# Expert jobs of 64 rows or fewer: the low parts of the activations beside the high parts

## The chip, the cores and the metric

One core of a Trainium2 chip runs the whole program. The metric is device time of one execution in microseconds, the median over runs. The matrix engine is TensorE (PE), the vector engine VectorE (DVE), the activation engine ScalarE (ACT), GpSimd is POOL, and SyncE (SP) issues the weight DMAs. Each engine has a sequencer that takes waits, branches and register loads and hands the rest to the engine's queue; the trace marks the sequencer's own instructions with a q (PEldq, DVEq).

## The reference

One decoder layer on x of 1 x 1024 x 1024 in float32: a combined projection, latent attention and differential attention, gates, an output projection, then a routed expert layer and a final norm. The change touches only the expert layer:

```
logits = t @ w_router + b_router;  top 4 of 32 experts for each of 1024 tokens
hcat = x_rows @ w1[e] + b1[e]                      # 1024 -> 2048
act  = min(glu, 7) * sigmoid(1.702 * glu) * (clip(lin) + 1)
y    = (act @ w2[e] + b2[e]) * weight of the row   # 1024 -> 1024
out[token] += y
```

Each expert has 4 MB in each half of w1 and 4 MB in w2, all in float32. For the reference's own inputs the router gives the 32 experts these numbers of rows, in order of size: 358, 240, 239, 227, 213, 196, 189, 183, 174, 170, 156, 136, 126, 124, 110, 110, 105, 100, 96, 92, 92, 91, 91, 81, 72, 68, 66, 56, 39, 35, 31, 30.

## The kernel before

`stage_experts` runs last. Its work is cut into jobs of one expert and up to 256 rows (JOB); the expert with 358 rows makes a second job of 102, so there are 33. The router's stage sorts them by rows, largest first, and writes tables that the engines read in their loops (`job_expert`, `job_count`, `job_place`). A job of more than 128 rows (P) is wide, the others are narrow: 12 wide jobs run first, then 21 narrow ones. Each engine loops over the jobs on its own, reads the counts into registers (`value_load`), and branches into a wide or a narrow body.

Weights. SP fills six slots of 2 MB for the next job (`load_weights`, lines 1817 to 1829). Slots 0 to 3 hold w1: slot c has 256 columns of the glu half and 256 of the linear half (s = 0 and 1), in two DMAs of 1 MB with rows of 1 KB. Slots 4 and 5 hold the halves of w2's columns, in one DMA of 2 MB each with rows of 2 KB. Each slot has one buffer: SP waits for the current job to be done with it (line 1915 for w1, by PE's count `made`, which rises eight times a job; line 1917 for w2, by `w_lo_ready`, which rises when DVE has split one of eight pieces of w2).

A narrow job on PE (`job`, line 2012). First projection, `first_narrow`: for c of 0 to 3 and s of 0 and 1, 16 plain float32 products with 128 columns, which the trace shows as 32 matmuls each, 256 in all. Its results go to the banks 2*(c%2)+s. Then eight transposes of the next job's rows (`turn_x`). Then the second projection with each operand split into a high and a low part (type fp32r): act_hi x w_hi, act_lo x w_hi and act_hi x w_lo, each of 16 matmuls 128x512, 48 in all, in eight pieces q of six (q 0 to 3 to bank 0, q 4 to 7 to bank 2). All matmuls take 128 stationary columns, however many rows the job has. A wide job does the same in 384 matmuls of 256 columns for the first projection and 96 or, at 192 rows (MID) or fewer, 80 for the second; those of 192 or fewer skip with a branch at each q (line 2054).

The pieces of w2. For each q ACT writes the high part (`high`, line 2119) and DVE the low part (`low`, line 2232). In a narrow job they go to six places (`narrow_slots[q % 6]`), so q 6 and 7 need the places of q 0 and 1: ACT waits on `piece_used`, which PE raises by one when it is through with q 0 and by one when through with q 1 (line 2062). PE waits before each q for `w_lo_ready` (line 2039), and at q 3 for the fourth `act_lo_ready`, which DVE gives when the low part of the last quarter of the activations is there (line 2271).

The end of a narrow job (`whole`): DVE scales bank 0 into yg, ACT scales bank 2, POOL scatters yg to the accumulated rows. PE's next job waits for `yg_dve` and `yg_act` before it writes the banks again (line 2022). After the last job, rows are read back, normed and stored.

Of the kernel before, what the change touches and what calls it, by code (L numbers as in the profile page):

```python
# [25 lines left out]
ALU = mybir.AluOpType  # L26
# [3 lines left out]
P = 128  # L30
# [1779 lines left out]

def weight_slots(g):

    return ([at(g, R + c * RING_SLOT, RING_SLOT).rearrange("p (s k n) -> p s k n", s=2, k=KT) for c in range(4)],
            [tiled(g, R + (4 + c) * RING_SLOT, FT, HALF) for c in range(2)])


def load_weights(g, io, eng, expert, slot):

    w1, w2 = weight_slots(g)
    if slot < 4:  # L1820
        src = io.w1.rearrange("e (k p) n -> p e k n", p=P)
        for s in range(2):
            col = s * D_EXP + slot * 2 * P
            eng.dma_start(w1[slot][:, s].unsqueeze(1), src[:, bass.ds(expert, 1), :, col:col + 2 * P]).then_inc(g.w_in[slot], 16)
    else:
        src = io.w2.rearrange("e (k p) n -> p e k n", p=P)
        col = (slot - 4) * HALF
        eng.dma_start(w2[slot - 4].unsqueeze(1), src[:, bass.ds(expert, 1), :, col:col + HALF]).then_inc(g.w_in[slot], 16)
# [28 lines left out]
def stage_experts(g, io):  # L1857
# [24 lines left out]
    first_of = lambda p: w1[p // 4][:, p // 2 % 2, :, p % 2 * P:(p % 2 + 1) * P]  # L1882
# [12 lines left out]
    with nc.Block() as block:  # L1895

        @block.sync
        def _(sp):
            sp.wait_ge(gathered, 32)
            for slot in (2, 3):  # L1900
                load_weights(g, io, sp, 0, slot)
            sp.wait_ge(scattered, 16 * TT)
            for slot in (4, 5):
                load_weights(g, io, sp, 0, slot)
            total = sp.value_load(g.total[0:1, 0:1], min_val=EXPERTS, max_val=JOBS)
            with sp.Fori(1, JOBS) as n:
                with sp.If(total > n):
                    expert = sp.value_load(g.job_expert[0:1, bass.ds(n, 1)], min_val=0, max_val=EXPERTS - 1)
                    for c in range(6):

                        if c < 4:
                            sp.wait_ge(made, 8 * n + (2 * c - 6))
                        else:
                            sp.wait_ge(w_lo_ready, 8 * n + (4 * c - 20))
                        load_weights(g, io, sp, expert, c)
                with sp.Else():
                    sp.nop()

# [65 lines left out]
        def _(pe):  # L1984
# [8 lines left out]
            def first_narrow(n, c, s):  # L1993
                for a in range(2):
                    for k in range(KT):
                        last = nc.tensor.matmul(bank(g, 2 * (c % 2) + s)[:, a * JOB:a * JOB + P], w1[c][:, s, k, a * P:(a + 1) * P],  # L1996
                                                xt[:, k, 0:P], start=(k == 0), stop=(k == KT - 1))
                last.then_inc(made, 1)

# [9 lines left out]
                        last.then_inc(slot_used.sem, 1)  # L2009
                last.then_inc(made, 1)  # L2010

            def job(n, wide, count, next_count):
                pe.wait_ge(xt_dve, 2 * n + 2)
                pe.wait_ge(xt_act, 4 * n + 4)
                for c in range(4):
                    pe.wait_ge(g.w_in[c], 32 * n + 32)
                    if c >= 2:
                        pe.wait_ge(act_ready, 4 * n + (c - 1))
                    for s in range(2):

                        if c < 2:
                            pe.wait_ge((yg_dve, yg_act)[c], 2 * n + (s + 1))
                        (first_wide if wide else first_narrow)(n, c, s)

                pe.wait_ge(gathered, 32 * n + 64)
                with pe.If(next_count > P):
                    turn_x(2)
                with pe.Else():
                    turn_x(1)


                halves = 2 if wide else 1

                if wide:
                    pe.sem_inc(piece_used, 2)
                pe.wait_ge(act_lo_ready, 4 * n + 3)
                for c in range(2):
                    for q in range(4 * c, 4 * c + 4):
                        pe.wait_ge(w_lo_ready, 8 * n + (q + 1))
                        if q == 3:  # L2040
                            pe.wait_ge(act_lo_ready, 4 * n + 4)
                        def second(h, x, y):
                            for a in range(2):
                                f = 2 * (q % 4) + a
                                last = nc.tensor.matmul(bank(g, 2 * c + h), x[:, f, h * P:(h + 1) * P], second_part(q, wide)[:, y, a, :],  # L2045
                                                        start=(f == 0 and x is act_hi and y == 0), stop=(f == FT - 1 and x is act_hi and y == 1))
                            return last

                        for h in range(halves):
                            second(h, act_hi, 0)  # L2050
                            if h == 0:
                                second(h, act_lo, 0)
                            else:
                                with pe.If(count > MID):
                                    second(h, act_lo, 0)
                            last = second(h, act_hi, 1)
                            if q % 4 == 3:
                                last.then_inc(y_made, 3 - halves)
                            elif wide and h == 1:
                                last.then_inc(slot_used.sem, 1)  # L2060
                            elif not wide and q < 2:
                                last.then_inc(piece_used, 1)

            pe.wait_ge(gathered, 32)
            turn_x(2)
# [1 line left out]
            with nc.Fori(0, JOBS, engines=[mybir.EngineType.PE], hint_back_edge=True) as n:  # L2067
                with pe.If(total > n):
                    count = pe.value_load(g.job_count[0:1, bass.ds(n, 1)], min_val=0, max_val=SEQ)
                    next_count = pe.value_load(g.job_count[0:1, bass.ds(n + 1, 1)], min_val=0, max_val=SEQ)  # L2070
                    with pe.If(count > P):
                        job(n, True, count, next_count)
                    with pe.Else():
                        job(n, False, count, next_count)
                with pe.Else():
                    pe.nop()

# [15 lines left out]
        def _(act):  # L2093
# [25 lines left out]
                nc.scalar.activation(second_part(q, wide)[:, 0], piece_of(q), ACT.Copy).then_inc(w_hi_ready, 1)  # L2119

            def first_high(n, p):
                if p % 4 == 0:
                    act.wait_ge(g.w_in[p // 4], 32 * n + 32)
                if p >= 4:
                    first_free(act, n, p - 4)
                nc.scalar.activation(first_part[p][:, 0], first_of(p), ACT.Copy).then_inc(v_hi_ready.sem, 1)  # L2126

            def job(n, wide, count, next_count):
# [43 lines left out]
                        nc.scalar.activation(yg[:, h, HALF:], bank(g, 2 + h), ACT.Copy, scale=weight(n, h)).then_inc(yg_act, 1 if wide else 2)  # L2172

                if not wide:
                    whole(1)
                    return
                with act.If(count > MID):
                    next_high()
# [34 lines left out]
        def _(dve):  # L2213
# [24 lines left out]
            def job(n, wide, count, next_count, expert):  # L2238
# [9 lines left out]
                for c in range(4):  # L2248
# [24 lines left out]
                    if wide:  # L2273
                        with dve.If(count > MID):
                            low_act(act_lo[:, fs, 0:JOB], slice(0, JOB)).then_inc(act_lo_ready, 1)
                        with dve.Else():
                            low_act(act_lo[:, fs, 0:P], slice(0, P))
                            low_act(act_hi[:, fs, MID:JOB], slice(P, MID)).then_inc(act_lo_ready, 1)
                    else:
                        low_act(act_lo[:, fs, 0:P], slice(0, P)).then_inc(act_lo_ready, 1)  # L2280
                    if not wide and c < 3:
                        low(n, 2 * c, False)
                        low(n, 2 * c + 1, False)
# [38 lines left out]
                        dve.wait_ge(yg_dve, 2 * n + 4)  # L2322
                        dve.sem_inc(low_added.sem, 1)
                else:
                    whole(1)
                    dve.sem_inc(low_added.sem, 2)

            dve.sem_inc(yg_dve, 2)
            first_low(0, 0)
# [81 lines left out]
```

## Time and profile before

| | |
|---|---|
| three runs | 2834.12, 2828.44, 2836.38 us; median 2834.12 us |
| the profiled execution | 2832.55 us, of which the span of the trace is 2830.9 us |
| PE busy | 2680.1 us, 95% of the span |
| DVE, ACT, POOL busy | 53%, 38%, 11% |
| granted clock of PE, mean | 0.975 of full |
| DMA | 527.28 MB, mean 186 GB/s |
| expert layer | from about 1121 us to about 2805 us; wide jobs to 1949 us, narrow jobs to 2797 us |

A matmul's duration in the trace holds its way through the array; the next one starts before it ends. What one costs in a stream is the distance between starts: the length of a piece of the chain of waits divided by its count. Every time is in us from the start of the span. In the timeline, "x48" merges 48 instructions, and the brackets at a row's end give the engine's idle time before it and what ended it.

### The profile page before, as it was taken

The page shows a single profiled execution, that of the slowest core. Times are in us where ns is not written, and L with a number is a line of the kernel's source. Part 1 is how long each engine was busy: PE and PEld are TensorE (multiplying, and loading weights), DVE is VectorE, ACT ScalarE, POOL GpSimd, SP SyncE. Part 2 cuts the span into 40 slices and gives each one's busy share as a digit, 9 for nine tenths or more (in the row PEclk, how much of TensorE's full clock was granted, in tenths as well). Part 3 has the DMA queues.
Part 4 walks back from the last instruction along what each step waited for, and adds up shares of the span by engine and source line. Part 5 has one row for each costly group of instructions (what it writes and reads, how often), then busy time and mean ns, then how long its engine had stood idle before and what let it go on. Part 6 is the DMA issues. An engine that isn't in the chain of part 4 may idle for free.

```text
span 2830.9 us, 46350 instructions
## 1 busy us (share of the span) xinstructions
PE 2680.1 (95%) x16420; PEld 2218.6 (78%) x16421; DVE 1503.9 (53%) x2641; ACT 1068.2 (38%) x1684; POOL 309.1 (11%) x327
## 2 busy tenths in 40 slices
PE   7899989979999997999999999999999999999995
PEld 3356655556666555899999999999999999999994
DVE  5545436764111246666666777775445544454444
ACT  2144324443110123545555555554333333333333
POOL 1000000000000124101111111110111211112111
PEclk9999989999999997999999999999999999999997
DMA  4000010002111552966666677767999999999995
GB/s 141 0 10 5 16 31 16 1 1 67 45 44 44 194 100 78 322 216 208 207 207 207 209 220 228 231 213 246 349 348 344 337 342 344 342 336 342 344 343 169
DMA packets 424683, 527.28 MB, mean 186 GB/s; under 512 B 27844, under 2 KB 334536, under 8 KB 424584
## 3 DMA queue, kind: packets, MB, share of 16 engines
q1 hardware_dynamic: 403544, 464.31, 50.6%
q0 software_dynamic: 20032, 62.11, 9.3%
q8 instruction: 37, 0.61, 0.1%
q14 instruction: 30, 0.25, 0.0%
q10 hardware_dynamic: 1040, 0.00, 0.0%
HBM read 482.23 MB, written 44.14 MB: 186 GB/s over the span
## 4 chain that ended last, share of the span: by engine, by line
PE 59%; DMA 1%; issue 0%; ACT 0%; SPq 0%; DVE 0%; POOLq 0%; POOL 0%; ACTq 0%
PE banks L1996 21%; PE banks L2006 20%; PE banks L2045 17%; PE banks L1988 1%; DMA arena<-acc_rows 0%; DMA acc_rows<-arena,rows 0%; ACT parts L2099 0%; SPq L1923 0%; DVE arena L2351 0%; ACT arena L2208 0%; ACT parts L2126 0%; ACT arena L2172 0%; POOLq L1949 0%; POOL acc_rows L1943 0%; ACT stat L2210 0%
## 5 line engine op out<-in xcount | busy, mean ns | idle before, releaser
L1996 PEld LDWEIGHTS banks<-arena 128*128 128x128 f32 x5376 | 603.5, 192 | 1.7
L1996 PE MATMUL banks<-arena 128*128 128x128 f32 x5376 | 603.7, 275 | 0.0
L2006 PE MATMUL banks<-parts 128*128 128x256 f32 x4608 | 558.6, 284 | 7.2 <-issue 7.2
L2006 PEld LDWEIGHTS banks<-parts 128*128 128x128 f32 x4608 | 557.9, 193 | 8.8 <-issue 8.0
L2045 PE MATMUL banks<-parts 128*128 128x512 f32 x2064 | 476.8, 391 | 0.0
L2045 PEld LDWEIGHTS banks<-parts 128*128 128x128 f32 x2064 | 385.1, 188 | 78.5
L2232 DVE TENSOR_TENSOR parts<-arena,parts 128x1024 fp32r<-128x1024 f32 x264 | 315.2, 1222 | 118.2 <-ACT parts L2119 118.0
L2255 DVE TENSOR_SCALAR arena<-banks,arena 128x128 f32<-128x128 f32 (+1 forms) x528 | 181.3, 392 | 317.6 <-PE banks L1996 314.0
L2236 DVE TENSOR_TENSOR parts<-arena,parts 128x1024 fp32r<-128x1024 f32 x192 | 233.6, 1224 | 183.9 <-ACT parts L2126 183.4
L2119 ACT ACTIVATE parts<-arena 128x1024 fp32r<-128x1024 f32 x264 | 269.2, 1055 | 77.4 <-PE banks L2006 43.4
L2126 ACT ACTIVATE parts<-arena 128x1024 fp32r<-128x1024 f32 x192 | 201.8, 1057 | 173.2 <-PE banks L2006 117.1
L1329 PE MATMUL banks<-parts 128*128 128x512 f32 x768 | 178.8, 393 | 0.0
L1329 PEld LDWEIGHTS banks<-parts 128*128 128x128 f32 x768 | 144.2, 188 | 33.3 <-issue 3.8
L2147 ACT ACTIVATE parts<-arena 128x256 fp32r<-128x256 f32 (+1 forms) x132 | 65.6, 497 | 257.5 <-DVE arena L2263 252.7
L2143 ACT ACTIVATE arena<-arena 128x256 f32<-128x256 f32 (+1 forms) x132 | 65.3, 495 | 229.9 <-DVE arena L2255 229.9
L1973 POOL COPY rows<-entries 128x2 int32 x33 | 6.0, 182 | 1092.3 <-ACT arena L2172 799.4
L1562 PE MATMUL banks<-arena 128*128 128x512 f32 x256 | 115.2, 609 | 6.0 <-PEq L1280 3.2
L1404 DVE TENSOR_TENSOR arena<-banks,arena 128x512 f32<-128x512 f32 x32 | 20.6, 686 | 184.1 <-ACT arena L1360 184.1
L1943 POOL DMA_INDIRECT acc_rows<-arena,rows x66 | 108.4, 1642 | 66.2 <-issue 66.2
L1321 PE MATMUL banks<-arena 128*128 128x512 f32 x256 | 111.3, 592 | 1.5 <-DVE arena L1384 1.5
L1562 PEld LDWEIGHTS banks<-arena 128*128 128x128 f32 x256 | 49.2, 195 | 66.9 <-issue 63.2
L1321 PEld LDWEIGHTS banks<-arena 128*128 128x128 f32 x256 | 48.5, 190 | 59.7 <-issue 59.2
(313 smaller groups left out, 2724.8 us busy)
## 6 DMA issues: line engine op xcount, KB each, us to landing
arena<-in_w SPq DMA_DIRECT2D x264, 1024.0 KB, 7.7
arena<-in_w SPq DMA_DIRECT2D x66, 2048.0 KB
arena<-in_w_in SPq DMA_DIRECT2D x27, 512.0 KB, 5.4
arena<-in_x SPq DMA_DIRECT2D x16, 512.0 KB, 7.0
h_rows<-arena POOLq DMA_DIRECT2D x10, 512.0 KB, 8.5
acc_rows<-arena SPq DMA_DIRECT2D x8, 512.0 KB, 5.3
arena<-acc_rows SPq DMA_DIRECT2D x8, 512.0 KB, 6.7
out<-arena SPq DMA_DIRECT2D x8, 512.0 KB, 6.8
```

Source lines behind the costliest of these rows:

```text
L1321: nc.tensor.matmul(bank(g, 4 * h + b), w[s][b][:, k, :], yt[:, k0 + k, cols], start=(k == 0), stop=(k == 3))
L1329: last = nc.tensor.matmul(bank(g, 4 * h + b), w_parts[:, s, c, b, k, :], part[:, k, cols], start=(k == 0 and c == 0 and part is h_hi), sto ...
L1562: last = nc.tensor.matmul(bank(g, 2 * (t % 2) + h), merged[:, k, t * P:(t + 1) * P], w_out[:, k, h * HALF:(h + 1) * HALF], start=(k == 0), ...
L1943: pool.indirect_dma_start(out=io.acc, out_offset=bass.IndirectOffsetOnAxis(ap=rows_out[0:rows, h:h + 1], axis=0), in_=yg[0:rows, h, :], in ...
L1996: last = nc.tensor.matmul(bank(g, 2 * (c % 2) + s)[:, a * JOB:a * JOB + P], w1[c][:, s, k, a * P:(a + 1) * P], xt[:, k, 0:P], start=(k == ...
L2006: last = nc.tensor.matmul(bank(g, 2 * (c % 2) + s)[:, a * JOB:(a + 1) * JOB], first_part[p][:, y, k, :], x[:, k, :], start=(k == 0 and y = ...
L2045: last = nc.tensor.matmul(bank(g, 2 * c + h), x[:, f, h * P:(h + 1) * P], second_part(q, wide)[:, y, a, :], start=(f == 0 and x is act_hi ...
L2119: nc.scalar.activation(second_part(q, wide)[:, 0], piece_of(q), ACT.Copy).then_inc(w_hi_ready, 1)
L2126: nc.scalar.activation(first_part[p][:, 0], first_of(p), ACT.Copy).then_inc(v_hi_ready.sem, 1)
L2232: nc.vector.tensor_tensor(part[:, 1], piece_of(q), part[:, 0], ALU.subtract).then_inc(w_lo_ready, 1)
L2236: nc.vector.tensor_tensor(first_part[p][:, 1], first_of(p), first_part[p][:, 0], ALU.subtract).then_inc(v_lo_ready.sem, 1)
L2255: nc.vector.tensor_scalar(dst[:, a, 0:w], bank(g, 2 * (c % 2) + s)[:, a * JOB:a * JOB + w], b1_t[:, bass.ds(expert, 1), s * FT + 2 * c + a ...
```

## The change

For narrow jobs of 64 rows or fewer, DVE writes the low parts of the activations into columns 64 to 127 of act_hi, which no row of the job uses. One pass act_hi x w_hi then gives hi x w_hi in the upper 64 output rows and lo x w_hi in the lower 64, act_hi x w_lo likewise, and ACT and DVE add the two halves at the end. The 16 matmuls act_lo x w_hi are skipped by a branch on the count, once for each half of the columns (at q 3 and q 7); for narrow jobs of 65 to 128 rows they run there, all eight of a half together. `piece_used` now rises by two, at q 3. The narrow body of PE no longer reads or tests the next job's count. w1's slots now hold 512 columns of one half of w1 each, with rows of 2 KB, and the waits on the slots follow.

```diff
-            col = s * D_EXP + slot * 2 * P
-            eng.dma_start(w1[slot][:, s].unsqueeze(1), src[:, bass.ds(expert, 1), :, col:col + 2 * P]).then_inc(g.w_in[slot], 16)
+        col = slot % 2 * D_EXP + slot // 2 * HALF
+        for ks in (slice(0, KT // 2), slice(KT // 2, KT)):
+            eng.dma_start(w1[slot][:, ks].unsqueeze(1), src[:, bass.ds(expert, 1), ks, col:col + HALF]).then_inc(g.w_in[slot], 16)
...
-                            sp.wait_ge(made, 8 * n + (2 * c - 6))
+                            sp.wait_ge(made, 8 * n + (4 * (c // 2) + c % 2 - 5))
...
-                    pe.wait_ge(g.w_in[c], 32 * n + 32)
                     for s in range(2):
+                        if c % 2 == 0:
+                            pe.wait_ge(g.w_in[c + s], 32 * n + 32)
...
-                with pe.If(next_count > P):
-                    turn_x(2)
-                with pe.Else():
+                if wide:
+                    next_count = pe.value_load(g.job_count[0:1, bass.ds(n + 1, 1)], min_val=0, max_val=SEQ)
+                    with pe.If(next_count > P):
+                        turn_x(2)
+                    with pe.Else():
+                        turn_x(1)
+                else:
                     turn_x(1)
...
+                        if not wide:
+                            if q % 4 == 3:
+                                with pe.If(count > P // 2):
+                                    for r in range(4 * c, 4 * c + 4):
+                                        second(c, 0, r, act_lo, 0)
+                            last = second(c, 0, q, act_hi, 0)
+                            if q == 3:
+                                last.then_inc(piece_used, 2)
+                            last = second(c, 0, q, act_hi, 1)
+                            if q % 4 == 3:
+                                last.then_inc(y_made, 2)
+                            continue
...
-                            elif not wide and q < 2:
-                                last.then_inc(piece_used, 1)
...   ACT, end of a narrow job
-                    whole(1)
+                    with act.If(count > P // 2):
+                        whole(1)
+                    with act.Else():
+                        for c in range(2):
+                            act.wait_ge(y_made, 4 * n + (2 * c + 2))
+                            nc.scalar.activation(low_sums[:, c * HALF:(c + 1) * HALF], bank(g, 2 * c)[P // 2:P], ACT.Copy).then_inc(yg_act, 1)
...   DVE, low parts of the activations
+                        with dve.If(count > P // 2):
+                            low_act(act_lo[:, fs, 0:P], slice(0, P)).then_inc(act_lo_ready, 1)
+                        with dve.Else():
+                            low_act(act_hi[:, fs, P // 2:P], slice(0, P // 2)).then_inc(act_lo_ready, 1)
...   DVE, end of a narrow job of 64 rows or fewer
+                        dve.wait_ge(yg_act, 2 * n + 3)
+                        nc.vector.tensor_tensor(low_sums[:, 0:HALF], low_sums[:, 0:HALF], bank(g, 0)[rows], ALU.add).then_inc(yg_dve, 1)
+                        dve.wait_ge(yg_act, 2 * n + 4)
+                        nc.vector.tensor_tensor(low_sums[:, HALF:], low_sums[:, HALF:], bank(g, 2)[rows], ALU.add).then_inc(low_added.sem, 1)
...
+                        nc.vector.tensor_scalar(yg[rows, 0, :], low_sums, weight(n, 0)[rows], None, ALU.mult).then_inc(yg_dve, 1)
```

## Rows read from the trace of the kernel before

**Rows 1.** The page: the whole span, and its costliest groups on PE.
```profile
span 2830.9 us, 46350 instructions
L1996 PE MATMUL banks<-arena 128*128 128x128 f32 x5376 | 603.7, 275 | 0.0
...
L2045 PE MATMUL banks<-parts 128*128 128x512 f32 x2064 | 476.8, 391 | 0.0
```

**Rows 2.** The chain that ended last, in order: start us, us, what.
```profile
1883.89 46.07 PE banks L2006 x384
1930.84 18.17 PE banks L2045 x80
...
2272.18 28.58 PE banks L1996 x256
2301.64 10.90 PE banks L2045 x48
2312.54 28.58 PE banks L1996 x256
```

**Rows 3.** Timeline of PE from 2300: start us, us, line, count.
```profile
2300.60 1.04 PE L1988 MATMUL banks<-ident,arena 128*128 128x128 f32 x8
2301.39 11.15 PE L2045 MATMUL banks<-parts 128*128 128x512 f32 x48
2312.38 28.75 PE L1996 MATMUL banks<-arena 128*128 128x128 f32 x256
```

**Rows 4.** Timelines of ACT and of DVE in the same job.
```profile
2303.68 2.02 ACT L2119 ACTIVATE parts<-arena 128x1024 fp32r<-128x1024 f32 x2
2312.73 0.69 ACT L2172 ACTIVATE arena<-banks,entries 128x512 f32<-128x512 f32 x1 [7.03 <-PE banks L2045]
...
2304.78 2.36 DVE L2232 TENSOR_TENSOR parts<-arena,parts 128x1024 fp32r<-128x1024 f32 x2 [0.89 <-ACT parts L2119]
2307.31 0.75 DVE L2304 TENSOR_SCALAR arena<-banks,entries 128x512 f32<-128x512 f32 x1 [0.17 <-PE banks L2045]
```

**Rows 5.** PE's sequencer, lines 2067 to 2071, 2022, 2041: ns min/median/max, first to last start.
```profile
L2067 PEldq ALU_OP  x1: 32/32/32, 2308.6 to 2308.6; - x1
L2070 PEldq FUSED_REGOPS  x2: 51/104/156, 2310.1 to 2310.6; - x2
L2071 PEldq COMPARE_BRANCH  x1: 216/216/216, 2310.9 to 2310.9; - x1
L2022 PEldq ALU_OP  x1: 32/32/32, 2311.5 to 2311.5; - x1
L2041 PEldq EVENT_SEMAPHORE  x2: 51/51/51, 2303.3 to 2343.6; - x2
```

**Rows 6.** PE at the second wide job's start, and its sequencer.
```profile
1203.31 1.14 PEld L2006 LDWEIGHTS banks<-parts 128*128 128x128 f32 x5 [5.37 <-issue]
L2003 PEldq FUSED_REGOPS  x1: 37/37/37, 1203.2 to 1203.2; - x1
L2003 PEldq ALU_OP  x4: 32/32/32, 1204.8 to 1215.2; - x4
```

**Rows 7.** Branches of PE's sequencer over the whole span.
```profile
L2054 PEldq COMPARE_BRANCH  x96: 71/148/218, 1175.3 to 1944.3; - x96
L2071 PEldq COMPARE_BRANCH  x45: 75/189/6157, 1124.0 to 2754.8; - x45
```

**Rows 8.** DMA from 2304 to 2308, from 2352 to 2356, and from 2300 to 2360.
```profile
DMA packets 1415, 1.43 MB, mean 358 GB/s; under 512 B 16, under 2 KB 1415, under 8 KB 1415
...
DMA packets 770, 1.54 MB, mean 386 GB/s; under 512 B 16, under 2 KB 16, under 8 KB 770
q0 software_dynamic: 395, 1.23, 8.0%
```

**Rows 9.** Timeline of SP from 2300: the weight DMAs.
```profile
2302.11 5.56 SPq L1828 DMA_DIRECT2D arena<-in_w  x2
2319.86 22.43 SPq L1824 DMA_DIRECT2D arena<-in_w  x8
```

**Rows 10.** End of a wide job of 192 rows or fewer, and POOL after a narrow job.
```profile
1883.93 0.59 ACT L2186 ACTIVATE arena<-banks 64x512 f32<-64x512 f32 x1
1884.56 1.28 DVE L2317 TENSOR_TENSOR arena<-arena,banks 64x512 f32<-64x512 f32 x2 [0.57 <-ACT arena L2186]
1885.97 0.74 DVE L2321 TENSOR_SCALAR arena<-arena,entries 64x1024 f32<-64x1024 f32 x1
1886.88 0.19 POOL L1973 COPY rows<-entries 128x2 int32 x1 [49.06 <-DVE arena L2321]
...
2313.64 0.18 POOL L1973 COPY rows<-entries 128x2 int32 x1 [24.00 <-ACT arena L2172]
```

**Rows 11.** The first job: DMA from 1131 to 1136, and ACT's wait for slot 3.
```profile
q0 software_dynamic: 244, 0.87, 87.0%
q1 hardware_dynamic: 245, 0.25, 17.8%
...
1156.92 2.01 ACT L2126 ACTIVATE parts<-arena 128x1024 fp32r<-128x1024 f32 x2 [2.09 <-DMA arena<-in_w]
```

More of the change, by code:

```diff
@@ L1811, in weight_slots @@
 def weight_slots(g):
-    return ([at(g, R + c * RING_SLOT, RING_SLOT).rearrange("p (s k n) -> p s k n", s=2, k=KT) for c in range(4)],
+    return ([tiled(g, R + c * RING_SLOT, KT, HALF) for c in range(4)],
             [tiled(g, R + (4 + c) * RING_SLOT, FT, HALF) for c in range(2)])
@@ L1821, in load_weights @@
         src = io.w1.rearrange("e (k p) n -> p e k n", p=P)
-        for s in range(2):
-            col = s * D_EXP + slot * 2 * P
-            eng.dma_start(w1[slot][:, s].unsqueeze(1), src[:, bass.ds(expert, 1), :, col:col + 2 * P]).then_inc(g.w_in[slot], 16)
+        col = slot % 2 * D_EXP + slot // 2 * HALF
+        for ks in (slice(0, KT // 2), slice(KT // 2, KT)):
+            eng.dma_start(w1[slot][:, ks].unsqueeze(1), src[:, bass.ds(expert, 1), ks, col:col + HALF]).then_inc(g.w_in[slot], 16)
     else:
@@ L1881, in stage_experts @@
     first_part = [slots[p % 4].rearrange("p (s k n) -> p s k n", s=2, k=KT) for p in range(W1_PIECES)]
-    first_of = lambda p: w1[p // 4][:, p // 2 % 2, :, p % 2 * P:(p % 2 + 1) * P]
+    w1_cols = lambda c, s, a: w1[2 * (c // 2) + s][:, :, (c % 2 * 2 + a) * P:(c % 2 * 2 + a + 1) * P]
+    first_of = lambda p: w1_cols(p // 4, p // 2 % 2, p % 2)
     second_part = lambda q, wide: (slots[q % 4] if wide else narrow_slots[q % 6]).rearrange("p (s f n) -> p s f n", s=2, f=2)
@@ L1995, in first_narrow @@
                     for k in range(KT):
-                        last = nc.tensor.matmul(bank(g, 2 * (c % 2) + s)[:, a * JOB:a * JOB + P], w1[c][:, s, k, a * P:(a + 1) * P],
+                        last = nc.tensor.matmul(bank(g, 2 * (c % 2) + s)[:, a * JOB:a * JOB + P], w1_cols(c, s, a)[:, k, :],
                                                 xt[:, k, 0:P], start=(k == 0), stop=(k == KT - 1))
@@ L2010, in first_wide, with job @@
                 last.then_inc(made, 1)
-            def job(n, wide, count, next_count):
+            def job(n, wide, count):
                 pe.wait_ge(xt_dve, 2 * n + 2)
@@ L2036, in job, with second @@
                 pe.wait_ge(act_lo_ready, 4 * n + 3)
+                def second(c, h, q, x, y):
+                    for a in range(2):
+                        f = 2 * (q % 4) + a
+                        last = nc.tensor.matmul(bank(g, 2 * c + h), x[:, f, h * P:(h + 1) * P], second_part(q, wide)[:, y, a, :],
+                                                start=(f == 0 and x is act_hi and y == 0), stop=(f == FT - 1 and x is act_hi and y == 1))
+                    return last
                 for c in range(2):
@@ L2041, in job @@
                             pe.wait_ge(act_lo_ready, 4 * n + 4)
[L2042 to L2047, printed above, removed]
+                        if not wide:
[10 more added lines that the diff above has]
+                            continue
                         for h in range(halves):
-                            second(h, act_hi, 0)
+                            second(c, h, q, act_hi, 0)
                             if h == 0:
-                                second(h, act_lo, 0)
+                                second(c, h, q, act_lo, 0)
                             else:
                                 with pe.If(count > MID):
-                                    second(h, act_lo, 0)
-                            last = second(h, act_hi, 1)
+                                    second(c, h, q, act_lo, 0)
+                            last = second(c, h, q, act_hi, 1)
                             if q % 4 == 3:
-                                last.then_inc(y_made, 3 - halves)
-                            elif wide and h == 1:
+                                last.then_inc(y_made, 1)
+                            elif h == 1:
                                 last.then_inc(slot_used.sem, 1)
-                            elif not wide and q < 2:
-                                last.then_inc(piece_used, 1)
             pe.wait_ge(gathered, 32)
@@ L2069, in _ @@
                     count = pe.value_load(g.job_count[0:1, bass.ds(n, 1)], min_val=0, max_val=SEQ)
-                    next_count = pe.value_load(g.job_count[0:1, bass.ds(n + 1, 1)], min_val=0, max_val=SEQ)
                     with pe.If(count > P):
-                        job(n, True, count, next_count)
+                        job(n, True, count)
                     with pe.Else():
-                        job(n, False, count, next_count)
+                        job(n, False, count)
                 with pe.Else():
@@ L2121, in first_high @@
             def first_high(n, p):
-                if p % 4 == 0:
-                    act.wait_ge(g.w_in[p // 4], 32 * n + 32)
+                if p % 8 in (0, 2):
+                    act.wait_ge(g.w_in[p // 8 * 2 + p % 8 // 2], 32 * n + 32)
                 if p >= 4:
@@ L2279, in job @@
                     else:
-                        low_act(act_lo[:, fs, 0:P], slice(0, P)).then_inc(act_lo_ready, 1)
+                        with dve.If(count > P // 2):
+                            low_act(act_lo[:, fs, 0:P], slice(0, P)).then_inc(act_lo_ready, 1)
+                        with dve.Else():
+                            low_act(act_hi[:, fs, P // 2:P], slice(0, P // 2)).then_inc(act_lo_ready, 1)
                     if not wide and c < 3:
@@ L2324, in job @@
                 else:
-                    whole(1)
-                    dve.sem_inc(low_added.sem, 2)
+                    with dve.If(count > P // 2):
+                        whole(1)
+                        dve.sem_inc(low_added.sem, 2)
+                    with dve.Else():
+                        rows = slice(0, P // 2)
+                        dve.wait_ge(yg_act, 2 * n + 3)
+                        nc.vector.tensor_tensor(low_sums[:, 0:HALF], low_sums[:, 0:HALF], bank(g, 0)[rows], ALU.add).then_inc(yg_dve, 1)
+                        dve.wait_ge(yg_act, 2 * n + 4)
+                        nc.vector.tensor_tensor(low_sums[:, HALF:], low_sums[:, HALF:], bank(g, 2)[rows], ALU.add).then_inc(low_added.sem, 1)
+                        dve.wait_ge(yg_free, n + 1)
+                        dve.wait_ge(yg_dve, 2 * n + 3)
+                        dve.wait_ge(low_added.sem, 2 * n + (low_added.count + 1))
+                        nc.vector.tensor_scalar(yg[rows, 0, :], low_sums, weight(n, 0)[rows], None, ALU.mult).then_inc(yg_dve, 1)
+                        dve.wait_ge(yg_dve, 2 * n + 4)
+                        dve.sem_inc(low_added.sem, 1)
             dve.sem_inc(yg_dve, 2)
```

## The prediction

> **What bounds the kernel now.** I read the page first, then the chain of waits, then the timeline of each engine over one narrow job, then the sequencer's own instructions on PE. The page shows PE's two big narrow groups with no idle time before them [rows 1]. The chain of waits is PE from the first job to the last, with no other engine in it: a narrow job is 28.58 us of first projection, 10.90 us of second, and some 0.9 us of transposes, 40.36 us from start to start, and each piece follows the one before without a hole [rows 2]. So only two things count: matmuls that leave PE, and holes that appear in PE. One matmul of the second projection costs 10.90 / 48 = 0.227 us, 18.17 / 80 in a wide job the same [rows 2].
>
> DMA is no bound, though the share reads full. A narrow job loads 12.58 MB: 8.39 MB in 1 KB rows at 358 GB/s and 4.19 MB in 2 KB rows at 386 GB/s, 23.4 + 10.9 = 34.3 us, and the gathers and scatters take 8.0% of the engines, 3.2 us a job [rows 8]: 37.5 of 40.36 us.
>
> **How many jobs.** The reference's router gives five experts 64 rows or fewer (56, 39, 35, 31, 30). Twelve have more than 128, and the second job of the largest is narrow, so 21 jobs are narrow: 16 of 65 to 128 rows and 5 short ones. The 2064 matmuls of line 2045 agree: 21 x 48 + 6 x 96 + 6 x 80 [rows 1].
>
> **Removed.** Sixteen matmuls in 5 jobs: 5 x 16 x 0.227 = 18.2 us less on PE, all on the path.
>
> **The new wait: pieces 6 and 7.** Before, PE gave back the places of pieces 0 and 1 after 6 and 12 matmuls, and DVE had both low parts done at 2304.78 + 2.36 = 2307.14 [rows 4], 5.75 us after PE began the second projection at 2301.39, while PE wants piece 6 only at matmul 36. Now PE gives both back at q 3: after 14 matmuls in a short job, after 22 in the others (12 + 8 low + 2). I count from PE's start, matmul i at 0.09 + 0.227 i (so the 48th is at 10.76, one step before the next job's first at 10.99 [rows 3]). An engine starts 0.6 us after the start of the matmul that frees it: ACT at 11.34 after the 48th, DVE at 5.92 after the 24th [rows 4]. DVE starts 1.10 after ACT and has both pieces 2.36 later [rows 4]. So the second low part is there at
> - short job: matmul 13 at 3.04, ACT 3.64, DVE 4.74, done 7.10. PE would be at piece 7 (after 28 matmuls) at 6.45.
> - other narrow job: matmul 21 at 4.86, ACT 5.46, DVE 6.56, done 8.92. PE would be there (after 36) at 8.26.
>
> PE's own time for piece 6 fits in between, so the second wait ends last. What is queued behind it is piece 7 and the whole next job.
>
> **What the wait uncovers: PE's sequencer.** Today it runs ahead. It reaches the loop's end at 2308.6, when the array has started 31 of 48 matmuls, so 16 pairs of weight load and matmul stand in the queue; from there to its last step before the next job (2311.5, plus some 0.05) it needs 2.95 us, of which the second count load is 0.8 (2310.1 to 2310.9) [rows 5]. The queue covers 3.6 us, so nothing shows. After a wait that has emptied the array, only what the sequencer hands over afterwards covers the loop. Its pace with an empty queue: 24 pairs between 1203.2 and 1204.8, some 0.0625 us a pair [rows 6] (the queue may have filled in that time, so this is an upper bound there; the bound above it that I keep is 0.11, the array's step in the first projection, 28.58 / 256 [rows 2]). With one load less the loop takes 2.15. A wait takes 0.05 [rows 5], a branch 0.07 not taken and 0.22 taken [rows 7], first weights 0.1 [rows 6].
> - short job: 7.10 + 0.05 + 0.22 + 4 x 0.0625 + 2.15 + 0.1 = 9.87 for the next job's first matmul, against 10.99: 1.12 us gained of the 3.63 removed.
> - other narrow job: 8.92 + 0.05 + 0.07 + 12 x 0.0625 + 2.15 + 0.1 = 12.04: 1.05 us lost. Its array is done at 8.92 + 0.22 + 12 x 0.227 = 11.86, so 0.9 of this is the piece and 0.2 the loop.
>
> The branch at q 3 costs nothing: the sequencer is held there for the fourth act_lo_ready until 2303.3, 1.9 in [rows 5], with some 4 of 12 matmuls still queued (0.9 us), and DVE's new branch before it is of the same size as PE's.
>
> **The end of a short job.** ACT copies 64x512 (0.59), DVE adds (half of 1.28) and scales (0.74) [rows 10]. From the last matmul: 0.6 + 0.6 + 0.04 + 0.68 + 0.05 + 0.75 = 2.7 us until yg_dve rises. PE wants it for s = 1 of the next job, 3.6 us after that job's start, so it hides; if DVE were over 2 us later it would cost the difference. Before, POOL started 1.5 us after the last matmul (2313.64 against 2312.15 [rows 4, 10]); now 2.7 + 0.17 = 2.9. This shows once, after job 33: 1.4 us more there. That job's last matmul comes at 8.15 instead of 10.76, so it gives 2.6 - 1.4 = 1.2.
>
> **Moved at no cost.** In wide jobs the next count is read after the first projection: 0.8 us of sequencer time under 16 queued pairs of 46.07 / 384 = 0.12 us [rows 2], 1.9 us; uncovered it would be at most 12 x 0.8 = 10 us. The test before a narrow job's transposes was covered in the same way, so its going gives nothing. Slots 0 and 2 of w1 are free one step of 3.57 us later, and slots 1 and 3 are wanted one step earlier. SP issued slot 0 at 2319.86, 7.5 us into the job [rows 9]; at 11 it still has 29 us until the next one. With 2 KB rows the weights take 12.58 / 386 = 32.6 us, 35.8 with the software queue, in a period of at least 39.2: the wide rows earn nothing now, and cover the shorter period. Slot 5 is issued 1 to 3 us later than before, behind slots 3 and 4 that are still moving. In the first job slots 2 and 3 share the engines with eight scatters, packet by packet (244 against 245 in 5 us [rows 11]). A 2 KB packet gets more of each turn; slot 3 lands by my estimate at 1151 instead of 1156.9, and ACT wants it at 1149 instead of 1155; PE's piece 10 comes at about 1157. No cost; 0 to 3 us if it lands no sooner.
>
> **Sum.** 16 x 1.05 - 4 x 1.12 - 1.2 = 16.8 - 4.5 - 1.2 = +11.1 us. On the profiled execution: 2832.55 + 11.1 = 2843.7. The median lies 1.6 above that execution, within its runs' spread of 8, so I forecast 2845. Its own range, for 0.3 us either way in a narrow job: 2839 to 2851.
>
> **Rivals.**
> - *The sequencer stays covered* (its loop is hidden in another way than by the queue). Then only pieces delay PE: others 8.92 + 0.22 - 8.26 = +0.88, short jobs 7.10 + 0.37 + 0.91 - 10.99 = -2.61. 16 x 0.88 - 4 x 2.61 - 1.2 = +2.5: 2837. For it: no hole is seen anywhere in 33 loops but one. Against it: the times of the sequencer. 0.2.
> - *The pieces are not late* (faster). PE's 10 matmuls between giving back and piece 6 last 2.27 us, ACT and DVE take 0.6 + 1.10 + 1.22 = 2.9 for the first piece. Should this chain be 0.9 us shorter than the rows say, all of it hides, and it is -18.2 + 1.4 = -16.8: 2817. Every row speaks against it. 0.12.
> - *A slower pace after a hole*: 0.11 us a pair, so 12 x 0.0475 in 16 jobs and 4 x 0.0475 in 4: +9.9, 2855. The first seconds of a stream are where the one pace I have was read. 0.18.
> - *A taken branch refetches code.* One branch took 6157 ns, the first jump to the loop's end; its neighbours take 75 to 189 [rows 7]. Ten new taken skips at that price, less 0.9 of cover at q 3: about 56 us, 2901. Against it: the taken ones among the 96 of line 2054 never took over 218 ns. 0.05. The Trainium skill ("Runtime: NRT & Kernel Launch", "Instruction fetch mechanics") says that a taken branch out of the window of fetched pages forces a DMA fetch before execution can go on. By that rule a skip over 16 instructions stays inside, and the trace agrees for skips of this length.
>
> **Chances.** The forecast has 0.45. No change means within 0.3%, 8.5 us, about what a measurement of this kernel can tell. Of the forecast's 0.45 I put 0.29 beyond 2842.6; with the slow pace and the refetch that is slower 0.52. Same: 0.16 + 0.18 = 0.34. Faster: 0.12, and 0.02 of the second. The range 2830 to 2860 leaves out the fast rival and the refetch.
>
> **What would show it.** On PE, holes before line 2045's successor: one or two a narrow job at pieces 6 and 7, with DVE's low part as releaser, in all 21. From start to start some 41.4 us in jobs of 65 to 128 rows and 39.2 in short ones. The sequencer's loop starts right after piece 7 is handed over, and a hole of 0.2 (others) or 1.6 us (short jobs) at the job boundary. DMA at about 386 GB/s in the weights. If the narrow jobs of over 64 rows still take 40.36 us, the piece step is wrong; if short jobs take 36.7, the whole saving came.

## The result, and the profile after

The changed kernel takes 2839.03 us (median of 20 runs, 2834.02 to 2841.64), the kernel before 2834.18 us beside it: ratio 1.002, 95% interval 1.0014 to 1.0025. It is 4.9 us slower, more than its measurement is uncertain, and less than the 0.3% that the prediction called a change. (Two of the twenty runs of the kernel before took 9.6 and 10.8 ms; they do not move the median.) The profiled execution has a span of 2837.3 us against 2830.9.

The page of the changed kernel: 80 matmuls are gone from the second projection (2064 to 1984 [rows 1]), 5 x 16, so five jobs are short.
```profile
span 2837.3 us, 46376 instructions
L1997 PE MATMUL banks<-arena 128*128 128x128 f32 x5376 | 604.1, 275 | 5.0 <-issue 5.0
...
L2046 PE MATMUL banks<-parts 128*128 128x512 f32 x1984 | 470.8, 394 | 4.8 <-issue 1.0
```

The chain of waits, one job of 65 to 128 rows and one short one (start, length, what). [Rows 2] had PE alone; now DVE's low part of piece 6 stands in it.
```profile
2318.99 28.58 PE banks L1997 x256
2348.45 5.02 PE banks L2046 x22
2354.58 1.24 DVE parts L2252
2355.86 1.21 PE banks L2046 x4
2357.10 3.01 PE banks L2046 x12
2360.11 28.58 PE banks L1997 x256
...
2645.78 28.85 PE banks L1997 x256
2675.51 3.20 PE banks L2046 x14
2679.82 1.24 DVE parts L2252
2681.10 1.20 PE banks L2046 x4
2682.51 1.20 PE banks L2046 x4
2683.70 1.24 issue
2684.95 28.85 PE banks L1997 x256
```
Read it as periods. Jobs of over 64 rows: 2360.11 - 2318.99 = 41.12 us, where it was 40.36. Short jobs: 2684.95 - 2645.78 = 39.17 us, the mean of the four 39.11 (the first is 38.90, since no hole precedes its first projection). In a short job 3.63 us of matmuls are gone and 1.2 of them are gained; "issue" is 1.24 us in which PE's queue is empty and the sequencer walks through the loop's end and head.

The same in the timelines (ACT, then DVE, in a job that began its second projection at 2348.20), against [rows 4]: ACT stood ready for 2.9 us before it had the places, DVE for 3.9.
```profile
2353.48 2.01 ACT L2134 ACTIVATE parts<-arena 128x1024 fp32r<-128x1024 f32 x2 [2.88 <-PE banks L2046]
...
2354.58 2.36 DVE L2252 TENSOR_TENSOR parts<-arena,parts 128x1024 fp32r<-128x1024 f32 x2 [3.88 <-ACT parts L2134]
```

PE's sequencer at the end of a job of over 64 rows and of a short one (ns min/median/max, first to last start), against [rows 5].
```profile
L2057 PEldq COMPARE_BRANCH  x2: 71/71/71, 2350.2 to 2357.0; - x2
L2088 PEldq COMPARE_BRANCH  x1: 186/186/186, 2357.2 to 2357.2; - x1
L2024 PEldq ALU_OP  x1: 32/32/32, 2359.5 to 2359.5; - x1
...
L2057 PEldq COMPARE_BRANCH  x2: 218/222/225, 2638.0 to 2643.1; - x2
L2088 PEldq COMPARE_BRANCH  x1: 190/190/190, 2643.4 to 2643.4; - x1
L2024 PEldq ALU_OP  x1: 32/32/32, 2645.7 to 2645.7; - x1
```
Line 2057 is the new branch, its second execution right after the wait for piece 7; line 2088 is the jump at the body's end. Between them lie 12 pairs of weight load and matmul in the first job and 4 in the second, and handing them over takes the sequencer at most 0.15 us. From the jump to the last step before the next job it is 2.3 us. Twelve matmuls cover that (2.7 us), four do not (0.9 us).

### The profile page after: what moved, and what is told of

The parts are those of the page before. It is cut to its first block, busy times and chain, and to the rows that moved or that the text cites. A ratio compares the mean times of both kernels' runs of the same rounds, so it can differ in the third digit from the quotient of the medians.

```text
span 2837.3 us, 46376 instructions
## 1 busy us (share of the span) xinstructions
PE 2675.7 (94%) x16340; PEld 2201.0 (78%) x16341; DVE 1505.6 (53%) x2651; ACT 1072.8 (38%) x1689; POOL 304.6 (11%) x327
## 4 chain that ended last, share of the span: by engine, by line
PE 56%; DMA 2%; DVE 1%; ACT 1%; issue 1%; SPq 0%; POOLq 0%; POOL 0%; DVEq 0%; ACTq 0%
PE banks L1997 21%; PE banks L2007 18%; PE banks L2046 15%; PE banks L1989 1%; DMA arena<-in_w 1%; DVE parts L2252 1%; ACT parts L2134 1%; DMA arena<-acc_rows 0%; DMA acc_rows<-arena,rows 0%; SPq L1924 0%; DVE arena L2387 0%; DVE arena L2275 0%; SPq L1824 0%; DVE parts L2256 0%; ACT arena L2228 0%
## 5 line engine op out<-in xcount | busy, mean ns | idle before, releaser
L2007 PEld LDWEIGHTS banks<-parts 128*128 128x128 f32 x4608 | 558.5, 193 | 8.4 <-issue 7.3
L2046 PEld LDWEIGHTS banks<-parts 128*128 128x128 f32 x1984 | 366.9, 188 | 95.4 <-DVE parts L2252 11.9
L1329 PEld LDWEIGHTS banks<-parts 128*128 128x128 f32 x768 | 144.2, 188 | 33.2 <-issue 3.8
```

Of the source, the lines that this page charges most:

```text
L1329: last = nc.tensor.matmul(bank(g, 4 * h + b), w_parts[:, s, c, b, k, :], part[:, k, cols], start=(k == 0 and c == 0 and part is h_hi), sto ...
```

## The experiments

Line numbers in the edits are left out. Each run was timed beside the kernel before, and its ratio is to that. Theories: *late pieces* (a low part comes after the array wants it) and *uncovered loop* (a late wait holds PE's sequencer, and the loop's 2.3 to 3.2 us show).

**Places given back early** (e1).
```diff
-    if q % 4 == 3:
+    if q % 4 == 3 or q == 1:
         with pe.If(count > P // 2):
-            for r in range(4 * c, 4 * c + 4): second(c, 0, r, act_lo, 0)
+            for r in range(q - 1 if q < 4 else 4, q + 1): second(c, 0, r, act_lo, 0)
...
-    if q == 3: piece_used += 2     # after the first pass
+    if q == 1: piece_used += 2     # after the last pass
```


> The changed kernel, but the low passes of pieces 0 and 1 run at q 1 (behind a branch of their own) and their places are given back there, after 12 matmuls (8 in a short job) in place of 22 (14). Late-places theory (all of the 0.77 us lost in each narrow job of over 64 rows comes from the chain give-back, ACT, DVE): those jobs are back at 40.36 us from start to start; a short job is then held only by PE's sequencer, which waits for the second low part at 5.8 us and has a taken branch and 2.4 us of loop behind it, so its successor starts at about 8.5 us after the second projection's start instead of 9.7 (period 38.0). In all 16 x 0.77 + 4 x 1.1 + 1.2 = 18 us less than the changed kernel: about 2821, 13 below the kernel before. Rival (the branch itself, or passes deferred behind it, cost the time, wherever the places are given back): no less than 2836, since there is one branch more.

Measured 2821.29 us, ratio 0.9953 (0.994 to 0.9967). Jobs of over 64 rows are back at 40.36 us, short ones at 38.12 (37.72 for the first), where 38.0 was expected. The loss in the 16 jobs goes with the places' late return; a third branch costs nothing there. In the short jobs no piece is late any more, yet a hole stays (chain of waits):
```profile
2624.79 7.27 PE banks L2046 x32
2632.05 1.00 issue
2633.05 28.85 PE banks L1997 x256
2661.90 0.87 PE banks L1989 x8
2662.77 7.29 PE banks L2046 x32
2670.06 1.11 issue
```

**Wide rows alone** (e2): the kernel before with the changed `weight_slots`, `load_weights` and their waits.

> The kernel before with only the weight slots changed: 2 KB rows for w1 and the waits that follow (slots free and wanted one step apart as in the change). Theory that DMA is no bound: no difference, within 2 us of the kernel before (2834), narrow jobs at 40.36 us, and the weight queue at some 386 instead of 358 GB/s. Rival (wide rows do gain, and hide a larger loss of the rest): 3 us or more faster. Rival (slots freed one step later or scatters slowed by larger packets cost time): 3 us or more slower.

Measured 2834.0 us, ratio 0.9999 (0.999 to 1.0008). The rows of 2 KB move faster (from 2304 to 2308, against 358 GB/s [rows 8]), all narrow jobs take 40.36 us, and PE waited for no weights. Only in the first job did ACT wait longer for slot 3, 6.1 us where it was 2.1.
```profile
DMA packets 773, 1.54 MB, mean 385 GB/s; under 512 B 22, under 2 KB 22, under 8 KB 773
```

**The load put back** (e3).
```diff
     count = pe.value_load(g.job_count[0:1, bass.ds(n, 1)], ...)
+    next_count = pe.value_load(g.job_count[0:1, bass.ds(n + 1, 1)], ...)
...
-    turn_x(1)                      # narrow body
+    with pe.If(next_count > P): turn_x(2)
+    with pe.Else(): turn_x(1)
```


> The changed kernel, but each narrow job loads the next job's count at its head and tests it before the transposes again, as the kernel before does. Uncovered-loop theory: in a short job the loop starts only when the second low part is there, so the load's 0.8 us show in full after each short job (period 39.17 to 39.95), and in the other narrow jobs all but the some 0.35 us for which 12 queued matmuls still cover (41.13 to 41.6). 4 x 0.8 + 16 x 0.45 = +10 us on the changed kernel: about 2849. Rival (the loop is covered in the jobs of over 64 rows by more than the trace tells): +3 us, 2842. Rival (the loop is covered everywhere): no difference, 2839.

Measured 2855.07 us, ratio 1.0079 (1.0065 to 1.0093), 16 us over the changed kernel. Both kinds of job feel it: 41.65 us (0.52 more), with a hole where there was none, and short ones with a hole of 2.0 to 2.1 in place of 1.25. I had not expected the rest: in three of the four short jobs the first projection then takes 30.48 us in place of 28.85.
```profile
2651.49 2.09 issue
2653.58 30.48 PE banks L1997 x256
```
The windows of this run show why (stretch; its length, PE busy, PEld, DVE, ACT, POOL, granted clock, DMA share, GB/s): soon after PE had stood idle for 2.1 us the granted clock fell to 0.50, that is 1.2 GHz, and some 3 us later it was back at 2.4 GHz.
```profile
2651.50:2653.50 2.00, 0.00 (x0) 0.00 (x0) 1.11 (x2) 0.59 (x1) 0.00 (x0) 1.00 1.05 388
2653.60:2655.00 1.40, 1.40 (x9) 1.40 (x10) 0.22 (x1) 1.28 (x1) 0.18 (x1) 0.72 1.04 386
2655.00:2656.50 1.50, 1.50 (x9) 1.50 (x9) 0.00 (x0) 0.00 (x0) 0.63 (x1) 0.50 1.04 385
2656.50:2658.00 1.50, 1.50 (x11) 1.50 (x10) 0.00 (x0) 0.00 (x0) 1.20 (x2) 0.62 1.05 389
2658.00:2660.00 2.00, 2.00 (x21) 2.00 (x20) 0.61 (x2) 0.14 (x1) 1.17 (x1) 1.00 1.05 387
```
16 x 0.52 + 4 x 0.8 + 3 x 1.63 = 16.4, which is the whole difference within what it can be measured to. The fall came after the holes of 2.09, 2.02 and 2.00 us and not after the one of 2.08, so the length of the hole alone does not decide it; after the changed kernel's holes of 1.25 us it did not come.

**Late places in the old order** (e7): the run that separates the two theories.
```diff
-    second(h, act_hi, 0)
+    last = second(h, act_hi, 0)
+    if not wide and q == 3: last.then_inc(piece_used, 2)
...
-    elif not wide and q < 2: last.then_inc(piece_used, 1)
```


> The kernel before with one thing changed: the places of pieces 0 and 1 are given back together at q 3, after its first pass (20 matmuls), nothing else. Here no piece comes too late for the array: the second low part is there at 8.5 us, and piece 7 has its turn at 9.6. But PE's sequencer is held at piece 7's wait until 8.5, where it used to hand over the last matmul at 7.2, and it needs some 3.15 us from there to the next job's first matmul (two loads; as in the run with the load put back). Sequencer theory: the next job starts at 11.75 in place of 10.99, a hole of some 0.75 us after each of 20 narrow jobs with PE's queue empty: +15 us, about 2849. Rival (only what is late for the array costs time; the sequencer hands waits to the queue and runs on): 40.36 us a job, 2834.

Measured 2850.73 us, ratio 1.0057 (1.0044 to 1.007): the uncovered loop. A period is 41.10 us. The matmuls of the second projection follow one another without a hole; the hole is behind them (timeline of PE):
```profile
2311.02 11.16 PE L2045 MATMUL banks<-parts 128*128 128x512 f32 x48
2322.64 28.85 PE L1996 MATMUL banks<-arena 128*128 128x128 f32 x256 [0.46 <-issue]
```
The low parts are done at 2316.96 + 2.36 = 2319.32, the jump at the body's end comes at 2319.4, 8.4 us into the projection (6.9 before: 2308.3 in the job that began at 2301.39), and the next job starts 3.2 us after it. With the hole come 0.27 us in the first projection (28.85 for 28.58), as after every hole.

**Late places, early load** (e9): the same, with the count kept in a register.
```diff
+    pe.reg_load(count_reg, g.job_count[0:1, bass.ds(n + 1, 1)])   # before turn_x
...
-    count = pe.value_load(...); next_count = pe.value_load(...)   # head of the loop
+    pe.reg_mov(now_reg, count_reg); count = pe.snap(now_reg)
```


> The run with late places in the old order (2851), with PE's count kept in a register and loaded before the transposes, so the head of the loop has no load. Sequencer theory: 1.6 us less between the wait's end and the next job's first matmul, 8.5 + 1.6 = 10.1 before 10.99: the hole of 0.46 us and the 0.3 us after it go in all 20 narrow jobs, 40.36 again, and with the second wide job's shorter hole about 2830. Rival (late places cost by themselves, DVE or ACT being later for the next job): 2845 or more.

Measured 2832.45 us, ratio 0.9993 (0.9984 to 1.0002). The places come back as late as before, and the periods are 40.36 us again (but for the first, which has a wait of its own, told of below). So what the run before lost in each job was the loop.

**The change with the early load** (e10): the same edit on the changed kernel.

> The changed kernel with PE's count kept in a register and loaded before the transposes. Theory: its narrow jobs of over 64 rows are held by the piece alone, the loop being covered by 12 matmuls, so they stay at 41.13 us; each short job's successor comes 0.8 us sooner (39.17 to 38.4). 4 x 0.8, and 2 to 3 us at the second wide job as in the candidate: 6 less than the changed kernel, about 2833. Rival (the loop holds the jobs of over 64 rows as well, the forecast's 0.2 us): 3 us more, 2830.

Measured 2834.49 us, ratio 1.0003 (0.9994 to 1.0012). Jobs of over 64 rows stay at 41.13 us: what they lose is the late piece alone, and the loop is covered. Short ones take 38.53, 0.6 less. The rest of the 4.5 us to the changed kernel lies mostly at the second wide job (see the candidate).

**No short jobs** (e8): `count > P // 2` becomes `count > 0` in all four places.

> The changed kernel with the threshold at 0 in place of 64 rows: no job is short, all 21 narrow jobs run the low passes behind the branches, the ends are as before. If the terms add up (0.77 us lost a narrow job of the long form; a short one 1.2 us gained against the kernel before and 1.9 against the long form): 21 x 0.77 = +16 us on the kernel before, 2851, and 11 to 12 above the changed kernel. Rival (the short jobs gain less because of what they share with the long ones, DMA above all): under 6 us above the changed kernel.

Measured 2849.66 us, ratio 1.0054 (1.0041 to 1.0067); all 20 periods are 41.13 us. The five short jobs are worth 10.6 us to the changed kernel, by the two medians.

**A candidate** (e5): one branch a narrow job, before the second projection, into a body with the old order and one with two passes a q; places given back after q 0 and q 1; the early load.
```diff
+    if wide: projection(False)
+    else:
+        with pe.If(count > P // 2): projection(False)
+        with pe.Else(): projection(True)
...
+    for x, y in ((act_hi, 0), (act_hi, 1)) if short else ((act_hi, 0), (act_lo, 0), (act_hi, 1)):
+        last = second(c, 0, q, x, y)
+    if q % 4 == 3: last.then_inc(y_made, 2)
+    elif q < 2: last.then_inc(piece_used, 1)
```


> A candidate: the changed kernel with one branch a narrow job into two bodies of the second projection. Jobs of over 64 rows have the order of the kernel before (hi, low, hi for each q), short ones two passes a q; places are given back after q 0 and q 1; and PE keeps the count in a register, loaded for the next job before the transposes, so the loop's head has no load. Both theories together: jobs of over 64 rows at 40.36 us; short ones wait for the second low part at 5.8 us, then 1.65 us of loop and 0.1: the successor at 7.6 us, where the 32 matmuls alone would give 7.4; period 37.0. 4 x 3.4 + 2.2 = 16 us less than the kernel before: about 2818. Should the loop not matter, 36.7 and 2817; should the register load in the middle of a job not be covered, 33 x 0.5 us more: 2834.

> The candidate once more, on the same chip as its form with 1 KB rows, to tell the two apart: 2816.

Measured 2815.8 us, ratio 0.9935 (0.9922 to 0.9949), and again 2815.86 us, 0.9934 (0.9921 to 0.9948): 18 to 19 us faster than the kernel before, and faster than the changed one. Periods 40.36 and 37.13 to 37.2 us (36.8 for the first short one).
```profile
2589.53 28.58 PE banks L1997 x256
2618.12 0.87 PE banks L1989 x8
2618.99 7.27 PE banks L2046 x32
2626.32 28.85 PE banks L1997 x256
```
Some 13 us of the gain are the four short periods. Two to four more lie at the second wide job, and the rest at the end of the last one. The second wide job starts behind a long branch with PE's queue empty. Here is that place in the chain of the kernel before, then of the candidate:
```profile
1198.37 4.95 issue
1203.32 48.64 PE banks L2006 x384
...
1197.01 3.39 issue
1200.40 46.33 PE banks L2007 x384
```
With two loads at the loop's head the hole is 4.9 us long (before, e2, e3, e7), with one 4.2 (the changed kernel, e1, e4, e8), with none 3.4 to 3.5 (e5, e6, e9 to e12). The first projection behind it takes 47.8 to 49.1 us in the first two groups and 46.3 to 47.8 in the third, where 46.07 is the rule [rows 2]: the granted clock is 0.50 in part of it, from 1201.8 to 1208.6 us in the kernel before and nowhere in it in the candidate's profile shown here. It differs from run to run by over 1 us, so it also makes the runs scatter.

**The candidate with the load at the loop's head** (e4).

> The candidate with the count loaded at the head of each job, and the next one in the middle of wide jobs, as the changed kernel has it. Sequencer theory: only jobs in which the queue is empty at the loop feel it. Short jobs: 0.8 us more after each of 4 (period 37.15 to 37.95), 3.2 us. The second wide job, whose start waits for a long branch: 0.8 us more, and some 2 us more if the longer hole brings PE's clock down, as it did in all runs with a hole of over 4 us there. The 27 others are covered: 0. Together 4 to 6 us: about 2821, like the run with early places. Rival (the early load saves in every job): 33 x 0.5, 2832.

Measured 2821.56 us, ratio 0.9957 (0.9944 to 0.997); short periods of 37.84 to 37.86 us (37.44 for the first), 0.7 more each. Jobs of over 64 rows stay at 40.36.

**The candidate with 1 KB rows** (e6), twice.

> The candidate (two bodies, early load) with the weight slots and the 1 KB rows of the kernel before. Its four short periods are 37.2 us, and the weights with gathers and scatters need some 37.5 us of DMA at 358 GB/s for the 1 KB rows. DMA-is-no-bound theory: the 20 us of lead that the slots give takes up 4 x 0.3 us, so no difference from the candidate, within 2 us of 2816. Rival (the wide rows carry the short jobs): PE waits on w_in in the last jobs, 3 us or more slower.

> The candidate with 1 KB rows once more. Its first profile had two waits that the candidate's had not, 1.2 us on the gather in the first narrow job and 1.1 us on a low part in the last. If the wide rows carry the shorter periods, both come again and it is 2 to 4 us slower than the candidate; if they were chance, the two are within 1 us.

Measured 2820.42 us, ratio 0.9951 (0.9938 to 0.9963), and 2818.34 us, 0.9945 (0.9932 to 0.9959). The intervals overlap those of the candidate, so the difference is not settled by the times; the waits are the same in both profiles (1.2 and 1.1 us, 1.3 and 0.9 us) and absent in both of the candidate. Those of PE in the first of them:
```profile
PE banks L1989 <- DMA arena<-h_rows,rows: 1.2, 1, 1.2
PE banks L2045 <- DVE parts L2298: 1.1, 1, 1.1
```
The first one is not the short jobs' doing: it comes in the first narrow job, sixteen jobs ahead of them, and the two runs with late places, which have 1 KB rows too, show it as well (1.1 and 1.8 us), while none with 2 KB rows does. The second one starts at the DMA. SP's issues for one job stretch out from short job to short job, which the waits on `made` alone would not do (in the candidate they stay at 18.79 us); in the last job ACT waited 6.6 us for w2.
```profile
2640.86 23.59 SPq L1824 DMA_DIRECT2D arena<-in_w  x8
2678.05 26.03 SPq L1824 DMA_DIRECT2D arena<-in_w  x8
2715.23 28.64 SPq L1824 DMA_DIRECT2D arena<-in_w  x8
```
I had forecast that the lead would take this up. It does not quite: at periods of 37 us loads in 1 KB rows fall behind by 1 to 3 us a job, which costs PE some 1 us after four such jobs. In the kernel before the wide rows alone earn nothing that its time shows.

## Why the prediction was right or wrong

The time lies in the range, on the forecast's side of zero, and 6 us below the forecast; the outcome held likeliest, slower by over 0.3%, did not come. The new wait and the loop behind it are what the runs show; two sizes in them were wrong. The range was wide enough to hold the rival without any loop as well (2837), and the time is nearer to that than to the forecast, so that it fell inside says little for the sizes. Point by point:

- *How many jobs, what leaves PE*: 80 matmuls, as counted.
- *The new wait*: shown. It appears in all 21 jobs and ends with the second low part, at 8.74 us in the long jobs (8.92 forecast) and 6.93 in the short ones (7.10). Giving the places back early takes it away and returns 40.36 us. But it isn't the late return alone: in the old order the same return makes no piece late. The pass order of the change, low passes in front of the return and fewer matmuls behind it, makes it late.
- *When ACT starts*: mis-sized. The forecast has ACT 0.6 us after the start of the matmul that frees it, read where ACT takes up a result [rows 4]; there ACT's sequencer has a wait and a register step of its own ahead of the instruction (at 2312.58 and 2312.63). When ACT waits for a place there are none, and it started 0.43 us after: 5.28 us into the projection in a long job (2353.48 - 2348.20) where 5.46 was forecast. DVE's 1.10 and 2.36 us are as forecast. This is the 0.17 to 0.18 us by which the second low part came sooner.
- *What the wait uncovers*: the mechanism is shown, its size was wrong. The sequencer hands over 12 pairs in some 0.1 us, not in 0.75. I took the pace from 24 pairs in 1.5 us [rows 6], and named it an upper bound, but carried it as the value; the queue had filled in that time. With it the loop's share of 0.2 us in jobs of over 64 rows goes: it is covered, by some 0.4 us (the load put back takes 0.8 us, and the next job's first matmul comes 12.17 us into the projection for 11.75). From the low part to that matmul it is 3.01 us, not 3.12. The long jobs lose 0.77 us and not 1.05, 4.5 us in sixteen: some 0.18 of each is the earlier start of ACT, some 0.1 the loop.
- *Short jobs*: the successor starts 9.69 us into the projection (9.87 forecast), and a period is 1.2 us shorter, where 1.12 was forecast. From the low part on the forecast was right to 0.01 us by luck: two errors cancel there, the faster handing over and a jump at the body's end that I had left out. The earlier start of ACT is what is left.
- *The end of the last job*: 1.0 us gained up to the scatter, 1.2 forecast. The spans differ by 6.4 us: the sixteen long periods give +12.0, the four short ones -5.0, the time after the last job's start -0.4 (reading the rows back took 0.5 longer), the time before the first narrow job -0.2.
- *Moved at no cost*: right for the wide rows and for eleven wide jobs' load; at the second wide job, where the queue is empty, one load less shortens the hole by 0.8 us (4.18 for 4.95). In the first job slot 3 landed at 1153.9, not at 1151; ACT waited 7.0 us for it, and the job took 0.6 us longer, within the 0 to 3 kept for it. The two about cancel.
- *Rivals*: the covered sequencer (2837) is true of the long jobs and false of the short ones, so the time lies between the two. No taken skip fetched code: all took 0.22 us. (The skips of line 2054 [rows 7] pass over two matmuls and their weight loads only; the long skip that the kernel before had, over sixteen transposes, took at most 0.23 us.) The slower pace is refuted.

## What to carry to other kernels

A matmul taken from a stream is worth its time only if what was hidden behind it still is; here the last 3.6 us of queued matmuls hid a loop's end and head as well as two conversions. Count what is queued behind the last wait of each iteration: the sequencer's loads and branches have just that long. Give a buffer back before the passes that can be deferred, and load what the next iteration branches on in the middle of this one.

## What the runs showed of the hardware

- A wait on PE holds its sequencer, not only the matmul behind it: with the array busy throughout, a wait that put the jump at the body's end 1.5 us later cost 0.74 us a job (41.10 for 40.36), and nothing once the loop had no loads.
- ACT started 0.43 us after the start of the matmul that freed a place for it, and 0.58 us after the one whose result it took up.
- With room in the queue the sequencer hands over 12 pairs of weight load and matmul in 0.15 us or less.
- The first products after an empty queue cost 0.27 us more (28.85 for 28.58 in 256), alike behind holes of 0.25, 1.25 and 2.08 us.
- Three idle stretches of PE of about 2.0 us, out of four, were followed by some 3 us at 1.2 GHz and cost 1.6 us each; the fourth, as long, was not, nor was any of four of 1.25 us.
- A stream in rows of 2 KB moved at 385 to 388 GB/s, in 1 KB rows at 358.
